# A two-block transformer kernel on one core: the first norm's root moved behind the first matmuls, and the bias table's write cut into four pieces

## The reference, cut to what matters

```python
def rmsnorm(x, gain):
    y = xf * lax.rsqrt(jnp.mean(xf * xf, axis=-1, keepdims=True) + NORM_EPS)
    return (y * gain.astype(jnp.float32)).astype(x.dtype)
...
        h = rmsnorm(x, g[0])
        y = hybrid_mixer(h, rel_bias_table, w_in[l], w_out[l], ...)
...
    z = h @ w_in
    za, zb, zc = jnp.split(z, [3 * A_WIDTH, 3 * A_WIDTH + 2 * B_WIDTH], axis=-1)
...
    zc = zc + (prev - zc) * mu
    r, k, v, w_lo, a_lo, g_lo = jnp.split(zc, cuts, axis=-1)
```

## Time and profile before

| what | us |
|---|---|
| median of 3 runs | 3176.25 |
| lowest, highest | 3176.15, 3180.94 |
| the profiled execution, its own time | 3177.01 |
| its span in the trace | 3175.2 |
| PE busy in it | 3039.0 (96%) |
| DVE busy | 1571.8 (50%) |
| ACT busy | 1267.2 (40%) |
| chain that ended last: PE, DVE, ACT, DMA | 87%, 6%, 3%, 3% |

### The profile page before, as it was taken

One profiled execution on the slowest core, in us unless ns is written; L12 is line 12 of the kernel. 1 busy time (PEld: TensorE's weight loads), 2 busy tenths in 40 slices (PEclk: granted clock), 3 DMA queues, 4 the chain that ended last, 5 costly groups with the idle time before them and its releaser, 6 DMA issues.

```text
span 3175.2 us, 52130 instructions
## 1 busy us (share of the span) xinstructions
PE 3039.0 (96%) x21592; PEld 2647.1 (83%) x21592; DVE 1571.8 (50%) x2406; ACT 1267.2 (40%) x1929; POOL 17.9 (1%) x34
## 2 busy tenths in 40 slices
PE   6999999899889999999998999999999999999997
PEld 6966666698779999999996888778878998889896
DVE  4444444544365556564445323554553474247754
ACT  3322112343445444443334223444442472245544
POOL 0000000000000000000000000000000000000000
PEclk9999999999989999999999999999999999999998
DMA  7568777544435555545553222222223443234342
GB/s 230 185 268 316 318 311 307 199 141 150 146 119 183 179 181 185 181 156 182 174 191 112 93 93 80 80 80 90 85 100 125 159 160 106 88 121 146 136 156 107
DMA packets 74280, 509.71 MB, mean 161 GB/s; under 512 B 8460, under 2 KB 8588, under 8 KB 20240
## 3 DMA queue, kind: packets, MB, share of 16 engines
q1 hardware_dynamic: 70416, 486.08, 42.9%
q0 software_dynamic: 3712, 21.40, 2.1%
HBM read 500.89 MB, written 6.55 MB: 160 GB/s over the span
## 4 chain that ended last, share of the span: by engine, by line
PE 87%; DVE 6%; ACT 3%; DMA 3%; issue 1%; SPq 0%; ACTq 0%; DVEq 0%
PE bank L685 40%; PE bank L1240 8%; PE bank L800 5%; PE bank L1271 5%; PE bank L1273 5%; PE bank L1272 5%; DMA high_f<-in_w_in 2%; PE bank L817 2%; PE bank L730 1%; PE bank L731 1%; PE bank L732 1%; PE bank L896 1%; PE bank L956 1%; DVE ring_f32r L1996 1%; PE bank L1309 1%
## 5 line engine op out<-in xcount | busy, mean ns | idle before, releaser
L1996 DVE TENSOR_TENSOR ring_f32r<-ring_f,high_f32r 128x1024 fp32r<-128x1024 f32 (+1 forms) x692 | 781.1, 1160 | 795.3 <-ACT high_f32r L1425 794.1
L1425 ACT CAST high_f32r<-ring_f 128x1024 fp32r<-128x1024 f32 (+1 forms) x692 | 655.8, 997 | 881.9 <-PE bank L685 536.2
L685 PE MATMUL bank<-y_f32r,high_f32r 128*128 128x256 f32 (+1 forms) x2784 | 853.1, 306 | 23.6 <-DVE ring_f32r L1996 11.2
L685 PE MATMUL bank<-h_f32r,high_f32r 128*128 128x256 f32 (+1 forms) x2208 | 685.8, 311 | 3.4 <-DVE y_f32r L1996 3.4
L685 PE MATMUL bank<-y_f32r,ring_f32r 128*128 128x256 f32 (+1 forms) x2208 | 673.9, 305 | 0.0
L685 PEld LDWEIGHTS bank<-y_f32r,high_f32r 128*128 128x128 f32 x2784 | 535.9, 192 | 47.4 <-issue 22.5
L685 PEld LDWEIGHTS bank<-h_f32r,high_f32r 128*128 128x128 f32 x2208 | 422.9, 192 | 25.3 <-issue 4.5
L685 PEld LDWEIGHTS bank<-y_f32r,ring_f32r 128*128 128x128 f32 x2208 | 424.9, 192 | 17.2
L1271 PE MATMUL bank<-h_f32r,high_f32r 128*128 128x512 f32 x512 | 209.3, 409 | 0.0
L800 PE MATMUL bank<-h_f,high_f 128*128 128x256 f32 x768 | 195.8, 393 | 11.1 <-DMA high_f<-in_w_in 10.9
L1273 PE MATMUL bank<-h_f32r,ring_f32r 128*128 128x512 f32 x512 | 200.1, 391 | 0.0
(11 more groups left out here) (415 smaller groups left out, 4960.1 us busy)
## 6 DMA issues: line engine op xcount, KB each, us to landing
ring_f<-in_w_in SPq DMA_DIRECT2D x135, 1024.0 KB, 4.9
ring_f<-in_w_mod SPq DMA_DIRECT2D x96, 1024.0 KB, 9.1
ring_f<-in_w_up SPq DMA_DIRECT2D x88, 1024.0 KB, 4.9
ring_f<-in_w_out SPq DMA_DIRECT2D x56, 1024.0 KB, 4.9
ring_f<-in_w_down SPq DMA_DIRECT2D x64, 704.0 KB, 4.1
high_f<-in_w_in SPq DMA_DIRECT2D x24, 1024.0 KB, 5.0
ring_f<-in_w_kv SPq DMA_DIRECT2D x8, 1024.0 KB, 5.0
ring_f<-in_w_q SPq DMA_DIRECT2D x4, 1024.0 KB, 4.8
```

The costliest lines, as they stand in the source:

```text
L685: last = mm(bk[(t0 + j) % banks][:, 0:width], w[:, c], x[:, k], start=(k == 0 and w is hi and x is rhs.hi), stop=(k == KC - 1 and w is lo))
L1425: act.copy(w_hi[p % 2][:, half], slot[s % SLOTS][:, half]).then_inc(w_high, 1)
L1996: return v.tensor_tensor(out, in0, in1, op)
```

## The change

The edits, all in the first 171 us:

- SP loads `vecs` ahead of x, and the first two slabs no longer wait for x.
- DVE makes `H[0]` = x times gain as the quarters land, without the root; the split and the first matmuls run on that. ACT squares x into `H[1]` behind the first slab's `high`; PE sums the squares between tiles 0 and 1 and finishes the sum within tile 1. DVE multiplies each output tile by the reciprocal root as it takes it from PSUM (it does the evacuation now, ACT does not), and scales `H[0]` itself in four steps behind tiles 8 to 11, for `projection1`.
- The two small matmuls of the bias table and of lambda move from before tile 0 to between tiles 4 and 5. DVE's copy of the lines and the small steps round it move behind the evacuation of tile 6.
- The bias table's write is four DMAs of three heads each: the first when the lines are there, the others when also 5, 10 and 15 tiles are done.
- The low-rank inputs are mixed in DVE's loop behind tile 20's evacuation; DVE then evacuates tiles 21 and 22 before the recurrence's first turn, and ACT applies tanh and sigmoid after its last `high`.

The diff, cut to what is spoken of:

```diff
@@ block.sync
             sp.dma_start(kbase, d["k_base"]).then_inc(S("base_loaded"), 16)
+            sp.dma_start(vecs, d["vecs"]).then_inc(loaded, 16)
             for q in range(4):
...
-            sp.dma_start(vecs, d["vecs"]).then_inc(loaded, 16)
...
-            sp.wait_ge(S("x_loaded3"), 16)
             for k in range(23):
+                if k == 2:
+                    sp.wait_ge(S("x_loaded3"), 16)
@@ block.gpsimd
-            pool.dma_start(d["skew"].rearrange("(h p n) -> h p n", p=P, n=384),
-                           g_line[0:A_HEADS, :].rearrange("h (a n) -> h a n", a=1).to_broadcast([A_HEADS, P, 384])
-                           ).then_inc(S("line_stored"), 16)
-            pool.wait_ge(S("line_stored"), 16)
+            for g in range(4):
+                if g:
+                    pool.wait_ge(gemm_done, TILE0["in1"] + 5 * g)
+                hs = slice(3 * g, 3 * g + 3)
+                pool.dma_start(d["skew"].rearrange("(h p n) -> h p n", p=P, n=384)[hs],
+                               g_line[hs, :].rearrange("h (a n) -> h a n", a=1).to_broadcast([3, P, 384])).then_inc(S("line_stored"), 16)
+            pool.wait_ge(S("line_stored"), 64)
@@ block.tensor
+            tile3("in1", 0, "in1", {}, RHS0["in1"])
             pe.wait_ge(S("base_loaded"), 16)
-            colsum4(H[0], T, 7)
+            all_sums[0] += 1
+            sums[0] += 4
+            for k in range(KC):
+                if k % 4 == 0:
+                    pe.wait_ge(sq_ready, k // 4 + 1)
+                part_sum(in1_sq, T, 7, k)
+            tile3("in1", 1, "in1", {3: lambda: finish_sum(T, 7)})
+            gemm3("in1", 2, 3, rhs="in1")
...
-            gemm3("in1", 0, 23)
+            gemm3("in1", 5, 18, rhs="in1")
@@ block.scalar
-            squares_of_x(0)
-            root()
+            rhs_highs("in1")
             high("in1", 0)
-            rhs_highs("in1")
+            for q in range(4):
+                f(in1_sq[:, 4 * q:4 * q + 4], X[0][:, 4 * q:4 * q + 4], ACT.Square).then_inc(sq_ready, 1)
             high("in1", 1)
...
+            for t in range(21):
+                act.wait_ge(gemm_done, t + 1)
+                high("in1", t + 2)
+                if t == 0:
+                    root()
...
+            lora_inputs()
+            act.wait_ge(gemm_free, 23)
@@ block.vector
-            rstd(D, RMS1_EPS, parts=True)
+            for q in range(4):
+                dve.wait_ge(S(f"x_loaded{q}"), 16)
+                for k in range(4 * q, 4 * q + 4):
+                    last = ts(H[0][:, k, :], X[0][:, k, :], gains(0)[:, k:k + 1])
+                last.then_inc(rhs_made, 1)
+                if q:
+                    rhs_low("in1", q - 1)
+            rhs_low("in1", 3)
             low("in1", 0)
-            rhs_made_and_split("in1", norm_quarter(H[0], X[0], gains(0)))
             low("in1", 1)
+            gather(T, 7)
+            low("in1", 2, halves=(0,))
+            rstd(D, RMS1_EPS)
+            for t in range(23):
+                dve.wait_ge(gemm_done, t + 1)
+                tt(Z[:, t + 26 if t < 21 else t + 3, :], bk[t % 2][:, 0:T], stat[:, 0:T]).then_inc(gemm_free, 1)
+                if t < 21:
+                    low("in1", t + 2, halves=(1,) if t == 0 else (0, 1))
+                if t == 6:
...
+                    v.tensor_copy(g_line[0:A_HEADS, :], bk[2][0:A_HEADS, 0:384]).then_inc(S("lam_line_made"), 1)
...
+                if 8 <= t < 12:
+                    c = slice(4 * t - 32, 4 * t - 28)
+                    step(tt(H[0][:, c], H[0][:, c], spread(stat[:, 0:T], 4)))
+                if t == 20:
...
```

More of the change, by code:

```diff
@@ L344, in build @@
         out1_sq = Z[:, 28:44]
+        in1_sq = H[1]
         rx = Area(X1_AT, KC * T)
@@ L721, in tile3 @@
                 pe.wait_ge(w_split, p + 1)
-                pe.wait_ge(gemm_free, n - 1)
+                if n > 1:
+                    pe.wait_ge(gemm_free, n - 1)
                 hi, lo = w_hi[p % 2], w_lo[sl % SLOTS]
@@ L1484, in squares_of_x @@
                     f(H[0][:, c], X[0][:, c], ACT.Square).then_inc(sq_ready, 1)
-            squares_of_x(0)
-            root()
+            rhs_highs("in1")
             high("in1", 0)
-            rhs_highs("in1")
+            for q in range(4):
+                f(in1_sq[:, 4 * q:4 * q + 4], X[0][:, 4 * q:4 * q + 4], ACT.Square).then_inc(sq_ready, 1)
             high("in1", 1)
-            act.wait_ge(S("line_lam_mm"), 2)
-            f(lam[:, 4:8], bk[3][:, 0:4], ACT.Exp).then_inc(S("lam_exp"), 1)
             def lora_inputs():
@@ L1499, in lora_inputs @@
                 act.copy(lora[1][64:P, :], Z[64:P, 44, :]).then_inc(S("rw_lora"), 1)
-            evac("in1", lambda t: at(Z, t + 3) if isinstance(t, int) and t >= 21 else at(Z, t + 26), n=23,
-                 between={22: lora_inputs})
+            for t in range(21):
[3 more added lines that the diff above has]
+                    root()
+                if t == 5:
+                    act.wait_ge(S("line_lam_mm"), 2)
+                    f(lam[:, 4:8], bk[3][:, 0:4], ACT.Exp).then_inc(S("lam_exp"), 1)
+            lora_inputs()
+            act.wait_ge(gemm_free, 23)
             def beside1(m, i, z):
@@ L2074, in gains @@
                 return vec("g")[:, n * KC:(n + 1) * KC]
-            dve.wait_ge(S("base_loaded"), 16)
             dve.wait_ge(loaded, 16)
             tt(lam[:, 0:4], vec("lamq"), vec("lamk")).then_inc(S("lam_line_made"), 1)
-            rstd(D, RMS1_EPS, parts=True)
+            for q in range(4):
[5 more added lines that the diff above has]
+                    rhs_low("in1", q - 1)
@@ L2110, in _ @@
-            dve.sem_inc(S("lora_mixed"), 1)
+            gather(T, 7)
[7 more added lines that the diff above has]
+                if t == 6:
+                    dve.wait_ge(S("lam_line_made"), 1)
+                    dve.wait_ge(S("line_lam_mm"), 1)
+                    v.tensor_copy(g_line[0:A_HEADS, :], bk[2][0:A_HEADS, 0:384]).then_inc(S("lam_line_made"), 1)
+                    dve.wait_ge(S("lam_exp"), 1)
+                    step(tt(lam[:, 8:10], lam[:, 4:6], lam[:, 6:8], ALU.subtract))
+                    for layer in range(2):
+                        init = 0.8 - 0.6 * math.exp(-0.3 * layer)
+                        step(ts(lam[:, 10 + layer:11 + layer], lam[:, 8 + layer:9 + layer], -1.0, -init))
+                        sub = vec("subln")[:, layer:layer + 1]
+                        step(ts(sub, sub, 1.0 - init))
+                    dve.wait_ge(S("mix_loaded"), 16)
+                    dve.wait_ge(S("sgu_loaded"), 9 * 16)
+                    step(tt(sgu_w, sgu_w, spread(kmix[:, 384:512], 8)))
+                    dve.sem_inc(S("sgu_masked"), 1)
+                if 8 <= t < 12:
+                    c = slice(4 * t - 32, 4 * t - 28)
+                    step(tt(H[0][:, c], H[0][:, c], spread(stat[:, 0:T], 4)))
+                if t == 20:
+                    dve.wait_ge(gemm_free, TILE0["in1"] + 21)
+                    dve.wait_ge(S("line_stored"), 64)
+                    v.memset(lora[0], 0.0)
+                    step(v.memset(lora[1], 0.0))
+                    for n in range(3):
+                        z = Z[:, 44 + n, :]
+                        tt(tmp[:, 1:T], z[:, 0:T - 1], z[:, 1:T], ALU.subtract)
+                        step(ts(tmp[:, 0:1], z[:, 0:1], -1.0))
+                        step(stt(z, tmp, vec("mulo")[:, n:n + 1], z, op1=ALU.add))
+                    dve.sem_inc(S("lora_mixed"), 1)
```

## The result

The changed kernel takes 3184.71 us (median of 17 runs, 3180.17 to 3187.76) against 3179.96 for the kernel before in the same comparison (17 runs, 3176.15 to 3184.13). The ratio is 1.0017 [1.001, 1.0023], 5.4 us more (3.2 to 7.3): a little slower, and inside the 0.2% (6.4 us) that were set as the bound of what can be told. The forecast was 3179.5, 3.3 us above the median then known, 3176.25. The kernel before stands 3.7 us above that median here, so the differences are compared, +5.4 with +3.3; by the bare number 3184.71 lies above the forecast's own range of 3174 to 3182 and within 3162 to 3187.

The account below looks back on a forecast made before the run. PE bounds the kernel, with one 11.1 us hole from the table's write. Opening -2.0, first pieces 0, fourth piece +4.0 and +1.3 sum to +3.3: 3179.5 us as median, own range 3174 to 3182, 8 in 10 within 3162 to 3187.

Parts of the forecast that it names:

- The bound: PE's largest hole in the 23 tiles, before tile 5, costs 8.2 + 2.9 = 11.1 us, caused by the table's write.
- Opening: Before tile 0: DVE's work there shrinks, tile 0 starts at 18.3 instead of 23.45; with work added to PE, -2.0 us.
- rival D: Opening edit fails: slab 0 or 1 comes late as POOL's loads compete; 0 instead of -2.0 us; no chance given.
- DVE's evacuation and the steps behind the tiles: In the run of tiles: the added DVE work fits into the 3 us DVE has free per tile; costs nothing.
- First turn of the recurrence: Near the run's end: DVE begins 4.4 us later, hidden by PE's 2.03 us weight-DMA wait; nothing, without that cover 1.
- Pieces one and two: Leave together behind tile 6, four lines share a source; hole of 8.2 plus 2.9 low clock near tile 11 or 12; change 0.
- Third piece: Issued behind tile 9: a slab delayed by 8.4 lands after 13.4, under 13.6, and the first hole covers it; 0.
- Fourth piece: Behind tile 14: three lines share, slab lands after 17.6; hole of 4.0 near tile 19, low clock 1.3 us.
- A: Rival: slabs pass the four write pieces and no hole remains; 3163 us, chance 0.28.
- B: Rival: the fourth piece's hole is as long as the first, with low clock in full; +9.1, 3185 us, chance 0.2.
- C: Rival: one smaller hole stays, the first pair's 2 to 5 us; 3168 to 3174 us, chance 0.1.
- Wrong if the four writes land in much less than 25 us: Sign against the forecast: the four pieces of the table's write each landing in much less than 25 us.

Follow-up runs that it names:

- experiment 5: Kernel before, opening untouched, with only the table's write cut into four pieces of 32 rows of all twelve lines: 3167.8 us, ratio 0.9967.
- experiment 2: Changed kernel with each write piece taking lines four apart (g, g+4, g+8) instead of three neighbours, at the same times: 3170.37 us, ratio 0.9973.
- experiment 8: Changed kernel with its neighbouring-line pieces set apart in time: first alone, second behind 12 tiles, last two together behind 17; 3186.47 us, a single execution.
- experiment 1: Changed kernel with the table's write as one DMA again, issued at the same place behind tile 6: 3177.84 us, ratio 0.9997.
- experiment 7: Changed kernel with the write in two pieces of 64 rows of all lines, at tile 6 and when 14 tiles are done: 3180.09 us, ratio 1.0006.

## Why the prediction was right, point by point

**The bound.** One hole of 8.2 us and 2.9 of low clock, caused by the write's queue: experiment 5 cuts that queue, leaves all else, and the run's end comes 10.75 us earlier, of 11.1 read. Confirmed.

**Opening, -2.0.** Tile 0 at 18.60, of 18.3; the part sums 1.93 and their end 0.60, of 1.9 and 0.6; the table's matmul and lambda's lie between 52.63 and 53.69, 1.06, of 1.0. Against the old start of tile 5 it is -1.9 in the changed kernel, and -1.9 at the run's end with one write. Confirmed in the run, rival D with it out; in the whole time no comparison resolves it.

**DVE's evacuation and the steps behind the tiles, 0.** Between 53.69 and the run's end PE is idle at the two holes only, and both end with a slab; without a write the 18 tiles take 103.80, 5.77 each. The cover held.

**First turn of the recurrence, 0 with a cover of 2.03.** DVE's scan, in the timeline of the changed kernel:

```profile
180.04 0.68 DVE L2168 TENSOR_TENSOR_SCAN y_f<-x_f,y_f 128x256 f32<-128x256 f32 x1
```

It moved from 175.05 by 5.0, the run's end by 4.4: DVE is 0.6 later, of 1 forecast, and PE still waits for the weight DMA, 1.41 instead of 2.03. Right, and by the cover that was named.

**Pieces one and two, no change against before.** They left together, as forecast, and a hole stands before tile 11. Its size was 7.47, of 8.2, and its low clock 1.8, of 2.9: 1.8 us too much in the sum. The mechanism is the one named: 0.7 of the 1.8 is the shorter hole, 1.1 the low clock, which was carried over from the old hole.

**Third piece, 0.** No idle by it. That it cost nothing because fewer lines share was not separated in this kernel, where the first hole overlaps it.

**Fourth piece, +4.0 and +1.3.** Here lies the term that was mis-sized the most. Place (tile 19), mechanism (three neighbours share a source) and direction were right; "16.8 x 3/4 = 12.6, landing after 17.6 us" was too low. It landed after 19.4, a delay of 14.4, and PE was idle 5.83; low clock was 2.2. That is 2.7 us more than the sum had. The step that failed is "16.8 x 3/4". Slabs issued some 5.5 us behind a piece were delayed by 3.4, 7.8, 14.4 and 16.8 to 17.9 us with one, two, three and four lines of a group queued: three have more than three quarters of the delay of four. How much of this is the proportion and how much the 16.8, one value out of the 16 to 19 that four lines gave in all, the runs don't part; three quarters of these are 12.1 to 14.3. And 1.3 for the low clock, read at another hole, was 0.9 too little.

The two errors partly cancel: 3.3 - 1.8 + 2.7 + 0.1 = 4.3, as in the account above. That the sum came so near is partly this luck; without it the forecast would have been off by up to 2.7. The rest of the way to the 5.4 us of the ratio is smaller than its interval.

**The rivals.** A named its condition rightly, lines of a piece on different sources, and experiment 2 is that case: 3170.37. But it put two sharing lines at 8.4 us of delay and found no hole, where 11.0 and a hole of 2.28 came out. B, a fourth hole as long as the first with its low clock in full, is nearer to what happened than it looked: 5.83 + 2.2 = 8.0 against the 9.3 of the first hole here. Its reason, that three lines are no faster than four, is nearly true of the delays (14.4 against 16.8). Its bare number, 3185, is that of the result, but by chance: it stands for +9.1 on 3176.25, and the difference measured, 5.4, is nearer to the forecast's 3.3. C did not occur. "Wrong if the four writes land in much less than 25 us": the fourth took 31.2; those of the other three can't be told apart in this kernel, only that the first three together were in flight from 69.5 to 111.8. In experiment 8 the first took 28.3 alone and the second, of which only two lines share, 22.0.

## What to carry to other kernels

A write that repeats a few partitions was slow at its source here and held engines that later, wide loads needed; what those loads met was the depth of the queue on the slowest engine. So cut such a write along the repeated dimension (here 32 rows of all lines, which alone brought the run's end of the kernel before 10.75 us forward), not between its partitions. If it must be cut between partitions, let a piece take partitions four apart. And before cutting, compare a load's landing time with what its buffers allow (13.6 us here): only what lies beyond is lost, but of that every microsecond, and low clock comes on top. Not tried here: a write with the repeated rows as its outer dimension, and a write issued at a time when no load follows.

## What the runs showed of the hardware that I had not expected

- The delay of a load by lines queued ahead grows with how many share a group of four partitions: 3.4, 7.8 to 11, 14.2 to 14.4 and 16 to 19 us for one to four, each read from one to a few slabs.
- It isn't proportional to the depth of the queue: 32 rows delay by 6.3 us, 64 by 13.5, 128 by 16 to 19. Between 64 and 128 queued rows more depth adds only 3 to 6 us to one load, since the load then shares the engines with the write; it lets more loads meet it.
- A piece of three neighbouring lines of one group, a quarter of the bytes, is in flight 28.3 to 31.2 us, the whole write 35.4 to 36.1. Three lines of which two share a group take 22.0, three lines four apart 16.7.
- Low clock behind these holes had its price: 1.8 us behind 7.47, 2.2 behind 5.83, 2.5 behind 8.91 (71.61 - 12 x 5.76, experiment 1). A hole of 4.90 had 2.3 behind it and one of 2.07 had 1.7 (25.32 - 4 x 5.76 and 30.54 - 5 x 5.76, experiment 7), but one of 2.28 only 0.3 (63.64 - 11 x 5.76, experiment 2). It doesn't grow in step with the hole.
